# Encoder block on eight cores: the last nine weight casts are released by the first group's mixers, read-backs get margins in SyncE's order, and the build-time planner assumes longer DMA times

## The reference, cut to what matters

```
h    = rms_norm(x, g_mix);  u = h @ w_in + b_in            # columns: GLU value | gate | q | k | v
conv = silu(layer_norm(depthwise_conv31(a * sigmoid(gate)) + b_dw))      # 512 channels
attn = banded attention of rotated q, k, v: 8 query heads, 2 kv heads, |i-j| <= 128, a sink logit
x   += concat(conv, attn) @ w_out + b_out
x   += memory_cross_attention(rms_norm(x), rms_norm(mem), w_mem_q, w_mem_kv, w_mem_o)   # 256 memory tokens
x   += (silu(h2 @ w_gate) * (h2 @ w_up)) @ w_down,  h2 = rms_norm(x),  2816 hidden columns
out  = rms_norm(x, g_final)
```

## Time and profile before

| what | us |
|---|---|
| runs shown: median (lowest, highest) | 2026.98 (2015.66, 2136.15) |
| the profiled execution's own time | 2019.87 |
| its span, first to last instruction, on core 3 | 2018.6 |
| spans of its other cores | 1975.7 to 2016.7 |
| TensorE busy | 1854.5 (92%) |
| VectorE, ScalarE, GpSimd busy | 1110.2, 872.1, 122.4 |
| DMA | 284.71 MB, mean 141 GB/s |

### The profile page before, as it was taken

How to read it: one execution, slowest core, us unless ns; L and a number is a source line. 1 busy time by engine, 2 the same in 40 slices (tenths; PEclk the granted TensorE clock), 3 DMA queues, 4 the chain that set the end, 5 groups by cost and what they waited for, 6 DMA issues and landing times.

```text
span 2018.6 us, 34398 instructions; the slowest of 8 cores (1975.7 to 2018.6 us)
## 1 busy us (share of the span) xinstructions
PE 1854.5 (92%) x11516; PEld 970.1 (48%) x11516; DVE 1110.2 (55%) x2430; ACT 872.1 (43%) x1761; POOL 122.4 (6%) x206
## 2 busy tenths in 40 slices
PE   3969998975775999999999999999999999999997
PEld 2535556842332544454454455445544544544443
DVE  4746665755353545754764485457547644754432
ACT  4534543543532453544455344535444553545210
POOL 2100000001001000000000000000000000000000
PEclk7989998977897999999999999999999999999999
DMA  8999864677079415331622353163316324521532
GB/s 246 185 205 196 203 157 153 150 202 227 0 128 151 142 48 200 133 120 58 230 105 82 124 205 118 50 213 131 108 58 230 105 80 131 178 100 58 188 141 100
DMA packets 80934, 284.71 MB, mean 141 GB/s; under 512 B 7159, under 2 KB 38777, under 8 KB 62872
## 3 DMA queue, kind: packets, MB, share of 16 engines
q1 hardware_dynamic: 73592, 237.74, 36.4%
q0 software_dynamic: 2560, 27.99, 9.8%
q10 hardware_dynamic: 4608, 16.78, 2.0%
HBM read 273.16 MB, written 65.10 MB: 168 GB/s over the span
## 4 chain that ended last, share of the span: by engine, by line
PE 76%; DMA 9%; issue 5%; DVE 5%; ACT 2%; SPq 1%; DVEq 0%; ACTq 0%; POOL 0%; POOLq 0%
PE bank L365 51%; PE bank L1430 15%; PE bank L373 5%; PE bank L774 2%; DMA arena<-s_y 2%; PE bank L1071 2%; SPq L355 1%; DMA arena<-w_in 1%; DMA arena<-s_gu 1%; DMA arena<-s_out 1%; ACT arena L386 1%; PE bank L1075 1%; DMA arena<-x 1%; DMA s_q<-arena 1%; PE bank L508 1%
## 5 line engine op out<-in xcount | busy, mean ns | idle before, releaser
L365 PE MATMUL bank<-arena 128*128 128x512 bf16 (+1 forms) x5724 | 1287.5, 377 | 23.4 <-ACT arena L1289 4.9
L365 PEld LDWEIGHTS bank<-arena 128*128 128x128 bf16 x5724 | 555.3, 99 | 629.8 <-issue 62.2
L1430 PE MATMUL bank<-arena 128*128 128x512 bf16 x1408 | 323.2, 379 | 0.6 <-DVE arena L1441 0.6
L386 ACT ACTIVATE arena<-arena 128x1024 bf16<-128x1024 f32 x130 | 137.2, 1056 | 309.8 <-DVE arena L1441 148.6
L1105 ACT ACTIVATE arena<-bank,asm 128x384 bf16<-128x384 f32 (+1 forms) x256 | 146.6, 573 | 157.4 <-DVE asm L1093 120.0
L1430 PEld LDWEIGHTS bank<-arena 128*128 128x128 bf16 x1408 | 133.7, 98 | 149.7 <-issue 7.5
L1396 ACT ACTIVATE arena<-bank 128x512 f32<-128x512 f32 x176 | 105.1, 597 | 214.1 <-PE bank L365 211.0
L373 PE MATMUL bank<-ident,arena 128*128 128x128 bf16 x2080 | 157.4, 224 | 39.1 <-DVE arena L632 15.3
L373 PEld LDWEIGHTS bank<-ident,arena 128*128 128x128 bf16 x2080 | 136.8, 100 | 85.4 <-issue 52.3
L1089 DVE TENSOR_REDUCE asm<-bank 128x1 f32<-128x384 f32 (+1 forms) x256 | 139.7, 546 | 57.2 <-PE bank L1075 49.8
L392 POOL TENSOR_TENSOR stat<-stat,mhalf 128x1 f32<-128x1 f32 x130 | 79.2, 610 | 1390.3 <-DVE stat L390 1354.9
(11 more groups left out here) (85 smaller groups left out, 1286.2 us busy)
## 6 DMA issues: line engine op xcount, KB each, us to landing
arena<-s_gu SPq DMA_DIRECT2D x88, 1024.0 KB, 6.0
arena<-x SPq DMA_DIRECT2D x64, 512.0 KB, 8.2
arena<-s_wd SPq DMA_DIRECT2D x32, 1024.0 KB, 4.9
out<-arena ACTq DMA_DIRECT2D x32, 512.0 KB, 3.7
arena<-s_wd SPq DMA_DIRECT2D x16, 768.0 KB, 4.6
s_gu<-w_gate_up POOLq DMA_DIRECT2D x11, 1024.0 KB, 10.2
s_mem<-w_memory POOLq DMA_DIRECT2D x8, 1024.0 KB, 13.6
arena<-s_mem SPq DMA_DIRECT2D x8, 1024.0 KB, 7.8
```

Of the source, the lines that this page charges most:

```text
L365: ins = nc.tensor.matmul(out_ap, l, r, start=(k == 0), stop=(k == n - 1))
L386: sc.op("act", lambda: nc.scalar.activation(junk, src, AF.Square, accum_out=st[:, 0:1]), reads=[srcb], writes=[junkb, stb], cost=1.26)
L1430: sc.op("pe", lambda t=t, bk=bk: nc.tensor.matmul(bk[:], actT[:, c, t * P:(t + 1) * P], w3[:, c - c0, :], start=(c == 0), stop=(c == NFC - ...
```

## The change

It does three things.

1. The call of `next_cast` in the channel mixer is taken out. A new function `pace(g)` makes that call for g = 0 in nine places of the first group's mixers: before each of the 4 output projections, before each of the 4 `s_mm`, and before tile 0's `p_tr`. Each is released by the operation recorded last before it. Casts 18 to 26 no longer wait for the third cast before them.
2. Operations get a `slack`, which the planner adds to the time at which one is ready. It changes no wait, only the place in the order: `load_vw` 14 us (the sixth 2 us), `mload` of units 0 and 1 8 us, and the q, k and v loads of `prefetch(0)` 30 us.
3. The planner's DMA costs: SP's issue 0.32 instead of 0.08 us, landing 3.0 us after the last byte instead of 2.0; the "hw" queue 300,000 bytes per us, or 180,000 while the "pool" queue is busy, instead of 330,000; the "pool" queue 235,000, or 150,000 while "hw" is busy.

```diff
@@ class Sched
-    ISSUE = {"sp": 0.08, "act": 0.1, "pool": 0.6}
+    ISSUE = {"sp": 0.32, "act": 0.1, "pool": 0.6}
@@ Sched.arrange
                 q = "pool" if e == "pool" else "hw"
-                rate = 235e3 if q == "pool" else 330e3
-                queue[q] = max(queue[q], t + o.cost) + o.nbytes / rate
-                end = queue[q] + 2.0
+                t0 = max(queue[q], t + o.cost)
+                busy = queue["hw" if q == "pool" else "pool"] > t0
+                rate = (150e3 if busy else 235e3) if q == "pool" else (180e3 if busy else 300e3)
+                queue[q] = t0 + o.nbytes / rate
+                end = queue[q] + 3.0
             for s in o.succ:
                 lat = 0.05 if (s.e == o.e and o.dma is None) else self.LAT[o.e]
                 s.ready = max(s.ready, end + lat)
                 s.left -= 1
                 if s.left == 0:
+                    s.ready += s.slack
                     wait[s.e].append(s)
@@ next_cast
-        rd = [scr_b[casts[k - 3][0]]] if k >= 3 else []
+        rd = [scr_b[casts[k - 3][0]]] if 3 <= k < 18 else []
         dma("pool", dst, src, rd, [scr_b[key]], DmaSem(nc, "cast%d" % k), after)
@@ load_vw
-        dma("sp", vws[k][0], full, [v_tile[n] for n in range(lo, vw_last[k] + 1)] + [v_pad], [vws[k][1]], vw_sem[k])
+        dma("sp", vws[k][0], full, [v_tile[n] for n in range(lo, vw_last[k] + 1)] + [v_pad], [vws[k][1]], vw_sem[k], (), 14.0 if k < 5 else 2.0)
@@ mload
-        dma("sp", ap, s_mem[u], [scr_b[("mem", u)]], [b_], mring_sem[k])
+        dma("sp", ap, s_mem[u], [scr_b[("mem", u)]], [b_], mring_sem[k], (), 8.0 if u < 2 else 0.0)
@@ prefetch
-            dma("sp", qT.rearrange("p a n -> p (a n)"), s_q[g], [q_g[g]], [qT_b], qT_sem)
+            dma("sp", qT.rearrange("p a n -> p (a n)"), s_q[g], [q_g[g]], [qT_b], qT_sem, (), 0.0 if g else 30.0)
...
-            dma("sp", kz[:, :, (b0 - lo) * P:(b1 - lo) * P], s_k[:, :, b0 * P:b1 * P], [k_g[k] for k in gs], [kz_b], kz_sem)
-            dma("sp", vz[:, b0 - lo:b1 - lo, :], s_vv[:, b0:b1, :], [vv_g[k] for k in gs], [vz_b], vz_sem)
+            dma("sp", kz[:, :, (b0 - lo) * P:(b1 - lo) * P], s_k[:, :, b0 * P:b1 * P], [k_g[k] for k in gs], [kz_b], kz_sem, (), 0.0 if g else 30.0)
+            dma("sp", vz[:, b0 - lo:b1 - lo, :], s_vv[:, b0:b1, :], [vv_g[k] for k in gs], [vz_b], vz_sem, (), 0.0 if g else 30.0)
@@
+    def pace(g):
+        if g == 0:
+            next_cast([sc.ops[-1]])
@@ out_proj
             def a():
+                pace(g)
                 st["b"] = proj(t, WO, [WO_b], lambda k: ymixT[:, k, t * P:(t + 1) * P], ymc_b + [yma_b[t]], True)
@@ mem_chain
             def s_mm():
+                pace(g)
                 st["s"] = proj(t, WK, WK_b, lambda k: ha[:, k, :], [hb], False)
...
             def p_tr():
+                if t == 0:
+                    pace(g)
                 bk, bkb = bank_p()
@@ f_steps, the up step
                 if c == NFC - 1:
                     note("gu", g)
-                if g == 0:
-                    next_cast([sc.ops[-1]])
```

More of the change, by code:

```diff
@@ L45 @@
 class Op:
-    __slots__ = ("e", "idx", "fn", "deps", "dma", "me", "waits", "signal", "cost", "nbytes", "n", "ready", "left", "succ", "start")
+    __slots__ = ("e", "idx", "fn", "deps", "dma", "me", "waits", "signal", "cost", "nbytes", "n", "slack", "ready", "left", "succ", "start")
 class Sched:
@@ L61, in __init__, with op @@
         self.sems = {e: nc.alloc_semaphore("prog_" + e) for e in self.ENG}
-    def op(self, e, fn, reads=(), writes=(), dma=None, cost=None, nbytes=0, after=(), touch=()):
+    def op(self, e, fn, reads=(), writes=(), dma=None, cost=None, nbytes=0, after=(), touch=(), slack=0.0):
         xr = [b for b in reads if b.excl and b not in writes]
@@ L81, in op @@
         o.nbytes = nbytes
+        o.slack = slack
         if dma is not None:
@@ L347, in give_p, with dma @@
         free_p.append((bk, bkb))
-    def dma(e, out, in_, reads, writes, sem, after=()):
+    def dma(e, out, in_, reads, writes, sem, after=(), slack=0.0):
         eng = {"sp": nc.sync, "act": nc.scalar, "pool": nc.gpsimd}[e]
@@ L354, in dma @@
         n *= 2 if in_.dtype == BF16 else 4
-        return sc.op(e, lambda: eng.dma_start(out=out, in_=in_), reads=reads, writes=writes, dma=sem, nbytes=n, after=after)
+        return sc.op(e, lambda: eng.dma_start(out=out, in_=in_), reads=reads, writes=writes, dma=sem, nbytes=n, after=after, slack=slack)
     def pe_cost(k, n):
```

## The result

The changed kernel is a little slower: the ratio of its time to that of before is 1.0058, with a 95% interval of 1.0042 to 1.0075 (medians 2034.05 and 2027.45 us of 12 runs each). The medians are of all runs, while every ratio here counts only runs in which neither die ran at a lower granted clock. By the 2% bound that is "the same"; I had forecast 1974 us, a gain of 2.6%. The profiled execution took 2038.63 us, its span 2037.4 on core 1.

The account below looks back on a forecast made before the run. It took TensorE's matmuls as the bound, with gains only where they wait: 2018.6 - 37.2 - 13 + 2 (k and v) + 1 (GpSimd) + 0 = 1971.4 us of span, forecast as 1974 us, range 1950 to 2005.

Parts of the forecast that it names:

- Part 1, the channel mixer: Group 0's channel mixer: without casts there, the group falls from 222.41 to 185.2 us, a gain of 37.2 us.
- my 90 us for the casts: Group 0's mixers: 10.5 MB of casts at 8.6 us each take 90 us, ending at about 569 us.
- Part 1, the new place: Group 0's mixers: casts fit, costing 0 (up to 10 us); GpSimd's issues cost 1 us (0 to 5).
- w_out: Load before the first output projection: its new order and cast 18 beside it change 0 us, between -6 and +6.
- the old hole: Group 0's channel mixer, 600 to 640 us: TensorE busy 16.87 of 40 us, casts colliding with ring and s_y loads.
- Part 2: Stage A: margins move q and s_v read-backs from in front of x loads, gaining 13 us (0 to 18.7).
- Rival A: Stage A is bound by transfers, not SP's order; only the mixer's hole closes, 1986 us; chance 0.17.
- My 18.7 us to be won: Stage A: TensorE's loss, 15.3 us in two waits plus 1.7 us of low clock after each.
- Part 3: SP's and other engines' order: the planner's new DMA times cost 0 us, between -5 and +8.
- B: Group 0's mixers: casts crowd GpSimd, a fourth or fifth in flight blocks its issue; 1987 us, chance 0.12.
- B's second sign: Group 0: the stretch from the first output projection to the channel mixer is longer than 77 us.
- C: Steady groups: the new order stalls each; at 10 us per group the time is 2043 us; chance 0.08.

Follow-up runs that it names:

- late_bn: Changed kernel with a 50 us margin on group 1's layer-norm statistics in VectorE's order; 1989.73 us, ratio 0.9835.
- no_casts: Changed kernel with part 1 undone: the nine casts back in the channel mixer, margins and planner times as changed; 2015.69 us, ratio 0.9943.
- casts_nofirst: casts_only without the cast release before the first output projection (tile 1's p_tr releases one more instead); ratio 0.9948.
- casts_only: Kernel before with part 1 alone, margins and planner times as before; 2022.7 us, ratio 0.9963.
- margins_only: Kernel before with the margins of part 2 alone, casts and planner times as before; ratio 1.0072.
- spread_only: Kernel before with stage A's casts released at other tiles, two fewer between tiles 2 and 8; 2014.69 us, ratio 0.9955.
- pace_mem: Changed kernel with the four cast releases before the output projections moved into the memory attention; 1986.82 us, ratio 0.9819.
- ring_later: Changed kernel with a 40 us margin putting the first four ring loads behind group 1's s_y loads; 2009.88 us, ratio 0.9943.
- mem_ring: pace_mem with the first four ring loads behind group 1's s_y loads; 1989.01 us, ratio 0.9835.

## Why the prediction was wrong

**Part 1, the channel mixer: right.** I had 185.2 us and a gain of 37.2; it is 184.85 us. By the mean of the cores the gain is 32.3 us: before, this stage took 208.8 to 222.7 us, and core 3, which I read, was near the top with 222.4. That nothing would be lost if the casts ran on into the channel mixer for some us held too (late_bn), though my 90 us for the casts were too few.

**Part 1, the new place: the step that failed.** I asked whether the casts would end before the channel mixer, and what GpSimd's issues would cost. I did not ask which loads of SP's queue run beside them from 479 us on, and who stands behind these. The rows for it were there: the earlier trace rows shows ring loads 3.6 times as slow beside casts, and I used it for w_out alone. The first two s_y loads of group 1 are issued at 477 us in the trace of before, and the four landed in a median of 6.8 us; VectorE's timeline has L1006 for them at 490, between two residual additions. I counted this term as nothing. It measured 51.7 us in the mixers by the mean of the cores (138.0 after, 86.3 in no_casts); with the 7.6 us of the new order alone it makes the 59.3. That s_y and a cast do harm each other I had even named as the cause of the old hole: the change moved this very collision, from a place where TensorE had other work left to one where a single chain runs.

**w_out: the mechanism right, the size not.** I took 0 with an end of +6 us. casts_nofirst shows the mechanism, and in casts_only the wait is 16.9 us on the slowest core, 12 more than the 4.98 of the earlier trace rows. In the kernel after it does not show, because there the new order issues w_out ahead of the ring loads and cast 18 comes behind its landing (464.04). Nor were the 6 us at the other end won: the first output projection now waits 6.9 us for VectorE's L1054 on every core, and B is no shorter (148.2 against 146.1).

**Part 2: wrong.** I took 13 us; the start of the convolution moved from 329.0 to 329.5 us. Though the reads of q and s_v had moved, x still came late (ScalarE waits 9.1 to 14.8 us for it on six of the eight cores, where it was 7.7 to 24.9 on all), and a second wait grew: VectorE's L670, which needs a buffer that a write of s_v must first have left, stands for 7.3 to 18.6 us, where it was 0 to 10.7. These are sums from 80 to 180 us; on core 5 of the kernel after, ScalarE's and VectorE's are

```profile
ACT arena L390 <- DMA arena<-x: 14.8, 2, 12.9
```

```profile
DVE arena L670 <- DMA s_v<-arena: 9.1, 1, 9.1
```

In margins_only the same instruction waits 9.2 to 15.0 us over the eight cores. So the margins had put off one transfer and another was late in its place. SP's blocked issue of 10.94 us did not go with the order either (in the kernel after an x load's issue takes 11.71 us at 116.67). Rival A was the right one, and spread_only shows it: with two casts fewer in the first tiles, and the 1 MB read-back of one of them later, ScalarE waits for x on no core, and L670 for 4.9 us at most, with SP's order all but unchanged. My 18.7 us to be won were core 3's own, too. Its convolution started at 337.3 us when the mean was 329.0; core 0's started at 316.5.

**Part 3: outside its bounds by itself, on the good side, and worse in company.** I had -5 to +8 us; alone it was 0.55% faster, 11 us of the slowest core's time, though the mean span of the cores in the profiled executions is 1.3 us longer (2005.7 against 2004.4), so the bounds did hold for the mean core. With part 1 it made the collision of part 1 larger by bringing 4 MB of ring loads to the same place. I had summed the parts as if they were independent.

**The rivals.** A held for stage A; but with it went the sum of 1986 us, which the freeze excluded. B's mechanism, GpSimd blocked by a fourth cast in flight, did not appear: GpSimd issued the fourth at 490.62 in 0.55 us. But B's second sign did, a stretch of more than 77 us from the first output projection to the channel mixer (138.0): that sign could not tell B from the freeze. C did not happen (175.92 of 177 us). The slower side came by a way not on my list, which is why the range of 1950 to 2005 left it out. Once the freeze is removed (late_bn, pace_mem), the ratios of 0.9835 and 0.9819 make 1994 and 1991 us on the scale of 2027.45, which is 17 to 20 us above the forecast of 1974: that one held 13 us of stage A as well, which never came. So the forecast was not simply that of a kernel without the freeze.

## What to carry to other kernels

Before a transfer is moved into an idle stretch, list every load that another queue issues in that stretch, multiply its landing by what the trace shows beside such transfers, and look on each in-order engine for the instruction that waits for it: an instruction that is early and not urgent is free only as long as its data is in time. Give such instructions, not only the loads, their margin in the order. And take a term that rests on a wait for DMA from all cores, not from the slowest.

## What the runs showed of the hardware

A queue of small packets got next to nothing beside one of large packets: 2.6% of the engines' time against 96.9% (ring_later, 480 to 500 us), while the packets of the two went nearly one for one (98 to 95, 490 to 510 us). The median landing of two 256 KB loads was 4.4 us when nothing stood ahead (ring_later), 7.4 us beside one cast (mem_ring), 22.0 us beside one cast and behind four ring loads (pace_mem), 37.8 us beside four casts (ring_later), 51.6 us beside four and behind the ring loads (after), and 73.3 us in late_bn, where casts kept coming. Seven casts in flight (late_bn, 506 us) did not hold up GpSimd, whose issues stayed at 0.49 to 0.57 us, while an issue of x on SP's queue took 11.71 us. What makes SP's issue take so long is not shown, and it is not the number of its transfers in flight alone: in the kernel before one took 10.94 us with three of them in flight, and in the kernel after one took 0.41 us with eleven.
